# Routing of a decoder trunk's mixture of experts: turning the residual, four rank products, first lists alone, lists of extra tiles between experts

## The chip, the cores and the metric

The kernel runs on one core of one Trainium2 chip. The metric is the device time of one launch in microseconds (us), the median of several runs. One run of the kernel was taken by the hardware profiler; all rows shown here come from it. PE is TensorE's matmul, PEld its weight load, DVE is VectorE, ACT ScalarE, POOL GpSimd; SP only starts DMAs.

## What is computed

One layer of a decoder trunk on 512 tokens (and 16 learned meta tokens ahead of them) of 1024 float32 values each. Three token mixers run side by side, their gated sum goes through an output product, and the result is added to the input. Then comes the part that this case is about:

```python
h = h + merged @ w_out                      # 512 x 1024
u2 = rmsnorm(h, norm_ffn)                   # h * rsqrt(mean(h*h) + eps) * norm_ffn
p_group = softmax(u2 @ wg + bg)             # 4 groups, the best one is taken
e_logits = (u2 @ we + be) of that group     # 8 experts, the best two are taken
e_w = the two best of softmax(e_logits), divided by their sum
y = sum over the two experts: g_val * e_w * (silu(u2 @ w_gate) * (u2 @ w_up)) @ w_down
out = rmsnorm(h + y, norm_final)
```

There are 32 experts with 1024 x 256 gate and up weights and 256 x 1024 down weights, 3 MB each and 96 MB in all. Each token goes to two of them.

## The kernel before, in words

**Order.** Five programs, one an engine, are written out by hand and joined by semaphores. They are a setup (the rows of x normed and turned, small constants as rows that one transpose turns into columns, L220 to L409), the three mixers (up to about 820 us of the span), and `tail()` (from L1592), in three parts: routing, experts, final sum. On each engine the instructions run in the order written. A `Steps` object counts an engine's steps by name; who needs a step waits for its count, so the order of the names is the order of the program.

**Routing, TensorE** (`tensor`, L1660 on). Token tile i (four of 128 tokens) has two output products `o{2i}` and `o{2i+1}`, each 8 matmuls of 512 columns into a PSUM bank of its own (L1684). Behind the products of tile i stand the router's logits of tile i-2 (`logits`, 8 matmuls of 36 columns, L1676) and the transposes of tile i-1 (`turn_tokens`, L1668), which turn rows of `u2`, the normed tokens. Behind the last products stand the transposes of tile 3 and the logits of tiles 2 and 3. The step `lg` is the last. Then come the ranks: which place a token has in its expert's list. A strictly triangular matrix and one of ones are multiplied by the 0/1 choices of each tile, 14 matmuls of 32 columns with the counts of each expert (L1698, L1700, L1702, step `rk`). Then 16 matmuls of 48 columns gather the table of token numbers by slot and by tile of 64 slots (L1708, step `tb`).

**Routing, VectorE** (`vector`, L1736 on). For each tile: add the products to `h` (L1750, 512 columns each), the sum of squares (L1753), mean and eps (L1755), wait for ScalarE's Ln and Exp (L1652, L1654), then the normed rows (L1761), and the copy of turned rows from PSUM to `u2T` (`turned`, L1744). After `lg` stands a chain of about 70 small instructions, each of which waits for the one before (helpers at L1767 to L1777): choice of group and experts up to `M`; ranks and counts read from PSUM; how many extra tiles of 64 rows each expert needs, and where they begin (`j64` to `ob`); places (`A1` to `oh`); eight one-hot matrices of slots (`sl0` to `sl7`, L1838); after `tb` the lists `xe`, `xo`, `xx` of rows to fetch and `yi` of rows to write; owners of extra tiles (`jb` to `ni`); and the weights of the two choices (`gs` to `c2`).

**Routing, queues.** SP starts `w_out`, x once more, the norm rows and the router's weights (L1637 to L1645), the weights of experts 0 to 2, keeps the normed rows of each tile in DRAM (`keep_rows`, L1947, semaphore `rows_kept`), and after `o7` starts the weights of expert 3, the rows of tile 3, and the weights of expert 4. When `rows_kept` shows all four tiles and the last transposes are done it starts the weights of expert 5.

**Experts.** Each expert has one tile of 64 rows; two experts make a pair of 128 rows. GpSimd waits for `rows_kept` and for `xo`, fetches the first two pairs by indirect DMA (L1931), and after `yi` the next two. TensorE turns a pair (L1965), makes gate and up products of an expert (`up`, 32 instructions, L1978), turns the hidden rows (L2013) and makes the down products (`down`, L1985). ScalarE has the sigmoid (L2043) and copies results out (L2049); VectorE copies turned pairs (L2071), gates (L2076, L2080) and copies hidden rows (L2086). GpSimd writes the results to DRAM by indirect DMA (L1937). Weights have six slots. SP loads gate and up of expert e+6 when `up(e)` is done (L1920), and ScalarE's queue loads its down weights after result e (L1923). Extra tiles (more than 64 rows for an expert) would run after all 32 experts, in loops that wait for the step `ni`; with these inputs none runs. The final part reads the results back, adds them weighted by `c_w`, norms and stores.

Of the kernel before, what the change touches and what calls it, by code (L numbers as in the profile page):

```python
# [25 lines left out]
NOWHERE = 65536.0  # L26
# [10 lines left out]
R_NORM, R_LB, R_AN, R_BN, R_CN, R_CONV, R_GKB = 0, 8, 12, 13, 14, 15, 63  # L37
NROWS = 65
# [13 lines left out]
def constants():  # L52
# [16 lines left out]
    j = np.arange(2 * NT)  # L69
    c[:, K_NUM:K_NUM + 2 * NT] = 1 + s + (j // 2 * P + j % 2 * SEQ)  # L70
    c[:, K_HALF] = np.arange(P) // SLOTS - 2
# [30 lines left out]
def hybrid_trunk(nc, x, meta_tokens, norm_mix, w_in, hgrn_lb_logits, hgrn_norm, gdn_conv, gdn_a_log,  # L102
# [4 lines left out]
    with ctx:  # L107
# [111 lines left out]
        def setup_sync(sp):  # L219
            sp.dma_start(xt[:, 0, :], xv[:, 0, :]).then_inc(sem("x_loaded0"), 16)  # L220
            sp.dma_start(C[:, 0:P], consts[:, 0:P]).then_inc(sem("ident_loaded"), 16)
            for at, src in ((R_NORM, norm_mix[0].rearrange("(a b) -> a b", b=P)),
# [3 lines left out]
                            (R_GKB, gla_gk_b[0].rearrange("(a b) -> a b", b=P))):  # L226
# [151 lines left out]
        def setup_tensor(t):  # L378
# [5 lines left out]
            for i in range(NT):  # L384
# [7 lines left out]
                if i == 0:  # L392
                    t.wait_ge(sem("rows_loaded"), 16 * 7)
                    t.transpose(bank(6, NROWS), rowsb, ident[0:NROWS, 0:NROWS]).then_inc(*pe0.did("rows"))
# [1199 lines left out]
        def tail():  # L1594
# [10 lines left out]
            pe2 = Steps(sem("router_pe"), ["o0", "o1", "o2", "o3", "T0", "o4", "o5", "T1", "o6", "o7", "T2", "T3", "lg", "rk", "tb"])  # L1605
            rt = ["lb", "gm", "lt", "ge", "gd", "gx", "og", "el", "es", "m1", "e1", "q1", "x1", "o1",
                  "n2", "m2", "e2", "q2", "x2", "o2", "dm", "O1", "O2", "M", "rank", "cnt",
                  "j64", "xa", "xb", "xc", "xd", "ci", "ob", "A1", "A2", "r1", "r2", "r3", "R1", "R1s", "R2", "R2s",
                  "pos", "pi", "pa", "pm", "tm", "oh"] + [f"sl{n}" for n in range(2 * NT)] + ["tz", "tg", "tx", "xe", "xo", "xx", "ty", "yi", "jb", "jc", "jd", "ji", "ni", "gs", "gv", "w1a", "w1", "w2", "c1", "c2"]
            rows_order = [step_ for i in range(NT) for step_ in ([f"h{2 * i}", f"h{2 * i + 1}", f"s{i}", f"ms{i}"] +  # L1610
                                                         ([f"T{i - 1}"] if i == NT - 1 else []) + [f"u{i}"] +
                                                         ([f"T{i - 1}"] if 0 < i < NT - 1 else []))] + [f"T{NT - 1}"]
            dve2 = Steps(sem("router_dve"), rows_order + rt)
            act2 = Steps(sem("router_act"), [f"{s}{i}" for i in range(NT) for s in ("ln", "rs")] + ["eg", "e2"])
# [32 lines left out]
            def scalar(a):  # L1647
                a.preload_act_table_set("natural_log_exp_and_others")
                for i in range(NT):
                    r = ss2[:, i:i + 1]  # L1650
                    a.wait_ge(*dve2.after(f"ms{i}"))
                    a.activation(r, r, ACT.Ln).then_inc(*act2.did(f"ln{i}"))  # L1652
                    a.wait_ge(*act2.after(f"ln{i}"))
                    a.activation(r, r, ACT.Exp, scale=-0.5).then_inc(*act2.did(f"rs{i}"))  # L1654
# [3 lines left out]
                a.activation(e2, dm, ACT.Exp).then_inc(*act2.did("e2"))  # L1658

            def tensor(t):  # L1660
# [3 lines left out]
                def turn_tokens(i):  # L1664

                    t.wait_ge(*dve2.after(f"u{i}"))
                    for k in range(KD):
                        mm = t.transpose(bank(2 * i + k // 4)[:, k % 4 * P:(k % 4 + 1) * P], u2[:, i, k * P:(k + 1) * P], ident)  # L1668
                    mm.then_inc(*pe2.did(f"T{i}"))

                def logits(i):
                    if i == 0:
                        t.wait_ge(sem("tail_small"), 96)
                    t.wait_ge(*dve2.after(f"T{i}"))
                    for k in range(KD):
# [3 lines left out]


                for i in range(NT):
                    for n in (2 * i, 2 * i + 1):
                        for k in range(KD):
                            mm = t.matmul(bank(n), gates[:, k, i * P:(i + 1) * P], wo[:, k, n % 2 * 512:(n % 2 + 1) * 512],  # L1684
                                          start=(k == 0), stop=(k == KD - 1))
                        mm.then_inc(*pe2.did(f"o{n}"))
                    if i >= 2:
                        logits(i - 2)
                    if i >= 1:
                        turn_tokens(i - 1)  # L1690
                turn_tokens(NT - 1)
                logits(NT - 2)
                logits(NT - 1).then_inc(*pe2.did("lg"))

                t.wait_ge(*dve2.after("M"))
                for i in range(NT):
                    dst = bank(3)[:, i * NX:(i + 1) * NX]
                    t.matmul(dst, strict, mm_[:, i, :], start=True, stop=(i == 0))  # L1698
                    for j in range(i):
                        t.matmul(dst, ones[:, :], mm_[:, j, :], start=False, stop=(j == i - 1))  # L1700
                for j in range(NT):
                    mm = t.matmul(bank(3)[:, NT * NX:(NT + 1) * NX], ones[:, :], mm_[:, j, :], start=(j == 0), stop=(j == NT - 1))  # L1702
                mm.then_inc(*pe2.did("rk"))

                for n in range(2 * NT):
                    t.wait_ge(*dve2.after(f"sl{n}"))
                    for half in range(2):
                        mm = t.matmul(bank(7)[half * SLOTS:(half + 1) * SLOTS, 0:NX + EXTRA], at_slot[:, n, :], at_tile[:, n, :],  # L1708
# [604 lines left out]
```

## Time and profile before

| | us |
|---|---|
| median of 3 runs | 1193.04 (1192.01 to 1194.77) |
| the profiled execution's own time | 1195.24 |
| its span | 1193.3 |
| TensorE busy | 1062.7 (89%) |
| VectorE busy | 482.8 (40%) |
| ScalarE busy | 309.6 (26%) |
| GpSimd busy | 58.9 (5%) |

Mean granted clock of TensorE: 0.952 of full. The span is what the profile's rows count from; the execution's own time is 1.94 us longer. Times in rows are us from the span's start.

### The profile page before, as it was taken

The numbers are of one execution on the slowest core, as the hardware profiler recorded it, in microseconds if no ns is written. First come the engines' busy times: TensorE is split into PE (matmuls) and PEld (weight loads), VectorE is DVE, ScalarE is ACT, GpSimd is POOL, SyncE is SP. The second block draws the span as 40 slices with busy tenths as digits, with TensorE's granted clock in tenths as the row PEclk, the third lists the DMA queues.
The fourth block names the chain that finished last, engine by engine and source line by source line (L and its number), as shares of the span: only waits on it lengthen the run. The fifth ranks groups of instructions, "written<-read, shape, count | busy, mean of one in ns | idle before, by whom it ended". The sixth has DMA issues, their size and how long they took to land.

```text
span 1193.3 us, 15437 instructions
## 1 busy us (share of the span) xinstructions
PE 1062.7 (89%) x6420; PEld 644.6 (54%) x6420; DVE 482.8 (40%) x988; ACT 309.6 (26%) x594; POOL 58.9 (5%) x67
## 2 busy tenths in 40 slices
PE   6999999989999999999989899898993999787870
PEld 5665665665585575675646546443463566444440
DVE  3536464537247256265254345422336212111115
ACT  2535445334233333234223023010000111101012
POOL 0000000000000000000000000000000122111110
PEclk9999999999999999999999899898985899988995
DMA  9222212232132131131122111064545799999965
GB/s 288 68 60 64 54 54 71 54 75 54 36 75 54 53 76 40 50 76 54 36 61 63 53 36 37 1 240 130 234 161 204 278 414 414 415 415 415 416 244 221
DMA packets 111689, 174.34 MB, mean 146 GB/s; under 512 B 8939, under 2 KB 86972, under 8 KB 103298
## 3 DMA queue, kind: packets, MB, share of 16 engines
q1 hardware_dynamic: 98354, 133.29, 32.4%
q10 hardware_dynamic: 7536, 28.90, 6.1%
q0 software_dynamic: 5728, 11.14, 3.8%
q8 instruction: 52, 0.85, 0.3%
q14 instruction: 19, 0.16, 0.0%
HBM read 169.09 MB, written 12.60 MB: 152 GB/s over the span
## 4 chain that ended last, share of the span: by engine, by line
PE 73%; DMA 13%; DVE 10%; ACT 2%; issue 1%; SPq 0%; POOL 0%; DVEq 0%; POOLq 0%
PE ps L732 22%; DMA arena<-in_expert_w_up 11%; PE ps L723 7%; PE ps L729 7%; PE ps L730 7%; PE ps L1978 5%; PE ps L1684 5%; PE ps L777 2%; PE ps L1985 2%; DVE arena L1269 2%; PE ps L756 1%; PE ps L786 1%; PE ps L1676 1%; DVE arena L1502 1%; DVE arena L1499 1%
## 5 line engine op out<-in xcount | busy, mean ns | idle before, releaser
L732 PE MATMUL ps<-arena 128*128 128x512 f32 x672 | 316.1, 606 | 7.2 <-DVE arena L1426 7.2
L732 PEld LDWEIGHTS ps<-arena 128*128 128x128 f32 x672 | 120.2, 191 | 122.8 <-issue 117.8
L729 PE MATMUL ps<-arena 128*128 128x264 f32 x416 | 129.0, 392 | 3.7 <-DVE arena L1426 2.9
L730 PE MATMUL ps<-arena 128*128 128x264 f32 x416 | 127.5, 388 | 0.0
L1978 PE MATMUL ps<-arena,gates 128*64 128x256 f32 x864 | 105.2, 399 | 22.5 <-DMA arena<-in_expert_w_up 21.0
L1269 DVE TENSOR_TENSOR arena<-arena 128x256 f32<-128x256 f32 (+6 forms) x194 | 91.6, 517 | 55.7 <-ACT arena L1090 35.4
L1978 PEld LDWEIGHTS ps<-arena,gates 128*64 128x64 f32 x864 | 64.0, 144 | 71.1 <-DMA arena<-in_expert_w_up 31.6
L723 PE MATMUL ps<-yT,arena 128*128 128x512 f32 x192 | 89.4, 622 | 2.2 <-DVE gates L1341 1.4
L729 PEld LDWEIGHTS ps<-arena 128*128 128x128 f32 x416 | 76.5, 191 | 19.9 <-issue 8.0
L730 PEld LDWEIGHTS ps<-arena 128*128 128x128 f32 x416 | 79.6, 191 | 13.8
L2071 DVE COPY gates<-ps 128x1024 f32<-128x1024 f32 x16 | 19.6, 1225 | 112.9 <-PE ps L1965 112.9
L723 PEld LDWEIGHTS ps<-yT,arena 128*128 128x128 f32 x192 | 37.5, 199 | 48.1 <-issue 47.6
L1684 PE MATMUL ps<-arena,gates 128*128 128x512 f32 x128 | 58.1, 615 | 5.5 <-DVE gates L1269 5.5
L777 PEld LDWEIGHTS ps<-arena 64*64 64x64 f32 x552 | 35.0, 134 | 31.6 <-DVE arena L1502 15.8
L1684 PEld LDWEIGHTS ps<-arena,gates 128*128 128x128 f32 x128 | 25.0, 198 | 37.1 <-issue 30.8
L777 PE MATMUL ps<-arena 64*64 64x64 f32 x552 | 40.5, 222 | 2.5 <-DVE arena L1502 2.4
L2043 ACT ACTIVATE gates<-ps 128x128 f32<-128x128 f32 x32 | 8.9, 278 | 130.2 <-PE ps L1978 130.2
L1985 PE MATMUL ps<-arena,gates 128*64 128x512 f32 x176 | 42.4, 604 | 0.0
L2076 DVE TENSOR_TENSOR gates<-gates,ps 128x128 f32<-128x128 f32 x32 | 9.0, 282 | 77.8 <-ACT gates L2043 77.8
L778 PE MATMUL ps<-arena 64*64 64x64 f32 x552 | 40.5, 222 | 0.0
L1931 POOL DMA_INDIRECT gates<-normed_tokens,gates x16 | 17.0, 1060 | 476.5 <-DVE gates L1774 408.8
L1273 DVE COPY_PREDICATED arena<-C,ps 128x512 f32<-128x512 int32 x56 | 39.6, 719 | 0.0
(327 smaller groups left out, 1281.8 us busy)
## 6 DMA issues: line engine op xcount, KB each, us to landing
arena<-in_w_in SPq DMA_DIRECT2D x68, 512.0 KB, 3.9
arena<-in_expert_w_gate SPq DMA_DIRECT2D x27, 1024.0 KB, 29.0
arena<-in_expert_w_up SPq DMA_DIRECT2D x27, 1024.0 KB, 33.9
arena<-in_expert_w_down ACTq DMA_DIRECT2D x18, 1024.0 KB, 33.1
arena<-in_w_branch SPq DMA_DIRECT2D x12, 512.0 KB, 3.9
C<-in_expert_w_gate SPq DMA_DIRECT2D x5, 1024.0 KB, 33.6
gates<-in_expert_w_up SPq DMA_DIRECT2D x5, 1024.0 KB, 38.9
arena<-in_w_out SPq DMA_DIRECT2D x1, 4096.0 KB, 14.3
```

The costliest lines, as they stand in the source:

```text
L723: mm = t.matmul(merge_bank[b], wt, rhs, start=first, stop=last)
L729: t.matmul(dst[:, 0:HALF], wt, uT[:, k, 0:HALF], start=(k == 0), stop=(k == KD - 1))
L730: mm = t.matmul(dst[:, HALF:], wt, uT[:, k, HALF:], start=(k == 0), stop=(k == KD - 1))
L732: mm = t.matmul(dst, wt, uT[:, k, META:], start=(k == 0), stop=(k == KD - 1))
L777: t.matmul(bank(n)[0:HP, at], lhs[0:HP, lo], rhs[0:HP, lo], start=True, stop=True)
L778: mm = t.matmul(bank(n + 1)[HP:, at], lhs[HP:, hi], rhs[HP:, hi], start=True, stop=True)
L1269: v.tensor_tensor(out_, a_, b2, op).then_inc(*q.did(name))
L1273: v.copy_predicated(tiles(pm), over(up(l).bitcast(I32), NT), tiles(src)).then_inc(*q.did(name))
L1684: mm = t.matmul(bank(n), gates[:, k, i * P:(i + 1) * P], wo[:, k, n % 2 * 512:(n % 2 + 1) * 512], start=(k == 0), stop=(k == KD - 1))
L1978: mm = t.matmul(dst, toks[:, k, :], src, start=(k == 0), stop=(k == KD - 1))
L1985: mm = t.matmul(bank(6 + b)[half * SLOTS:(half + 1) * SLOTS, :], hT[b][:, j * SLOTS:(j + 1) * SLOTS], weights[n][1][:, at:at + 512], start ...
L2071: v.tensor_copy(xT[q % 2], ps[:, 0:2 * 512].rearrange("p (k t) -> p k t", k=KD)).then_inc(pair_read.sem, 1)
```

## The change

- The transposes turn `h`, the residual, in place of the normed rows. The router's weights are multiplied by `norm_ffn` once (step `wn`; the column form comes from one more DMA of 8 rows in the setup, transposed with the others: 73 rows for 65), and the logits by each token's factor after their products (step `sc`). The sum of squares goes from VectorE to ScalarE as `Square` of 1024 columns with an accumulator.
- TensorE's order: `o2`, turn 0, `o3`, `o4`, logits 0, turn 1, `o5`, `o6`, logits 1, turn 2, six of the eight matmuls of `o7`, the first half of turn 3, the other two, logits 2, the second half of turn 3, logits 3 in two halves.
- The normed rows of tile 3 are made after `M`; ScalarE's queue, not SP's, keeps them in DRAM, after `e2`.
- Ranks: one product of 128 columns with the triangular matrix and three with ones, of 96, 64 and 32 columns, for `rk`. The four products of counts go to another bank and step, `ct`, behind it.
- Places: `rk` and `pos` give each choice's rank directly, two instructions `sl0`, `sl1` of 256 columns make the eight one-hot matrices, and the right operand of the table is the 0/1 choices times the token's number (`num`). Ranks of 64 and above match no slot. The table has 32 columns. Lists: `vi`, `xe`, `xo`, `yi`.
- Weights of choices, counts, extra tiles' places and lists stand in the experts' program of VectorE, between its steps; the 16 products of the extra table stand in TensorE's behind the down products of expert 7. ScalarE no longer waits for `ni` ahead of its first sigmoid.

The diff's core:

```diff
-NOWHERE = 65536.0
+NOWHERE = 4 * SEQ
@@ setup_sync
+                            (R_FFN, norm_ffn[0].rearrange("(a b) -> a b", b=P))):
@@ scalar
+                    a.wait_ge(*dve2.after(f"h{2 * i + 1}"))
+                    a.activation(scr2, h[:, i, :], ACT.Square, accum_out=r).then_inc(*act2.did(f"sq{i}"))
...
+                a.wait_ge(*dve2.after(f"u{NT - 1}"))
+                a.dma_start(u2_dram[(NT - 1) * P:, :], u2[:, NT - 1, :]).then_inc(sem("rows_kept"), 16)
@@ tensor
+                out_product(6, every).then_inc(*pe2.did("o6"))
+                logits(1, every, "t1")
+                turn_tokens(2, every, "T2")
+                out_product(7, range(0, KD - 2))
+                turn_tokens(3, low_half, "T3a")
+                out_product(7, range(KD - 2, KD)).then_inc(*pe2.did("o7"))
+                logits(2, every, "t2")
+                turn_tokens(3, high_half, "T3b")
+                logits(3, low_half, "t3a")
+                logits(3, high_half, "t3b").then_inc(*pe2.did("lg"))
...
+                t.matmul(rank, strict, mm_, start=True, stop=False)
+                for i in range(1, NT):
+                    mm = t.matmul(rank[:, i * NX:], ones[:, :], mm_[:, 0:(NT - i) * NX], start=False, stop=(i == NT - 1))
+                mm.then_inc(*pe2.did("rk"))
                 for j in range(NT):
+                    mm = t.matmul(bank(4, NX), ones[:, :], mm_[:, j * NX:(j + 1) * NX], start=(j == 0), stop=(j == NT - 1))
+                mm.then_inc(*pe2.did("ct"))
@@ vector
+                residual(0)
+                residual(1)
+                for i in range(1, NT):
+                    residual(2 * i)
+                    turned(i - 1)
+                    normed(i - 1)
+                    if i == NT - 1:
+                        turned(i, 0)
+                    residual(2 * i + 1)
+                turned(NT - 1, 1)
...
+                tt("num", numbered, by_expert, NUM.unsqueeze(2).broadcast_to([P, 2 * NT, NX]), ALU.mult)
+                normed(NT - 1)
                 v.wait_ge(*pe2.after("rk"))
+                tt("rk", ranked.rearrange("p (k i) e -> p k (i e)", k=2), chosen, over(bank(3, NT * NX), 2), ALU.mult)
+                red("pos", pos, ranked, ALU.add)
+                for k in range(2):
+                    slots_of(f"sl{k}", slice(k * NT, (k + 1) * NT), pos)
                 v.wait_ge(*pe2.after("tb"))
+                held = bank(7, NX)
+                ts("vi", vi, held, -1.0, ALU.mult, float(NOWHERE), ALU.add)
+                ts("xe", xi[0:SLOTS, 0:NX // 2], vi[0:SLOTS, 0:NX:2], WHERE, ALU.bitwise_and)
+                ts("xo", xi[SLOTS:P, 0:NX // 2], vi[SLOTS:P, 1:NX:2], WHERE, ALU.bitwise_and)
+                ts("yi", yi[:, 0:NX], held, -2.0, ALU.mult, C[:, K_HALF:K_HALF + 1], ALU.add)
@@ esync
                 load_weights(sp, 3, 3)
-                keep_rows(NT - 1)
                 load_weights(sp, 4, 4)
                 sp.wait_ge(sem("rows_kept"), 16 * NT)
-                sp.wait_ge(*pe2.after(f"T{NT - 1}"))
+                sp.wait_ge(*pe2.after("T3b"))
                 load_weights(sp, 5, 5)
@@ etensor
                     down(e)
+                    if e == 7:
+                        t.wait_ge(*dve2.after("et"))
+                        for n in range(2 * NT):
+                            for half in range(2):
+                                mm = t.matmul(bank(5)[half * SLOTS:(half + 1) * SLOTS, 256:256 + EXTRA], at_slot[:, n, :], at_tile[:, n, :],
+                                              start=(n == 0), stop=(n == 2 * NT - 1))
+                        mm.then_inc(sem("extra_table"), 1)
@@ evector
+                weights_of_choices()
                 read_pair(0)
+                extra_tiles()
                 read_pair(1)
+                first_extra_tile()
                 hidden(0)
                 hidden(1)
                 read_hidden(0)
...
+                        if e == 7:
+                            extra_lists()
                         hidden(e + 2)
                     read_hidden(e + 1)
+                    if e == 0:
+                        extra_places()
+                    if e == 1:
+                        extra_slots()
+                    if e == 2:
+                        extra_owners()
```

## Rows read from the trace of the kernel before

**Rows 1.** Busy time, granted clock, DMA share, GB/s by stretch: late routing and experts
```profile
core 0: us, PE busy (x) PEld busy (x) DVE busy (x) ACT busy (x) POOL busy (x), PEclk, DMA share, GB/s
910.00:915.00 5.00, 0.00 (x0) 0.00 (x0) 4.42 (x18) 0.00 (x0) 0.00 (x0) 0.50 0.01 2
925.00:930.00 5.00, 3.52 (x18) 2.34 (x18) 1.23 (x1) 0.00 (x0) 0.99 (x1) 0.50 0.21 57
1050.00:1100.00 50.00, 40.48 (x294) 24.40 (x294) 7.27 (x18) 4.41 (x11) 9.11 (x9) 0.86 1.02 415
```

**Rows 2.** Chain of work that ended last (start, us, what): first and last weights
```profile
927.63 5.80 PE ps L1978 x32
...
1109.94 44.00 DMA arena<-in_expert_w_up
```

**Rows 3.** The same chain: transposes and logits beside the output products
```profile
851.28 0.87 PE ps L1668 x8
...
865.89 1.71 PE ps L1676 x16
...
887.36 1.78 PE ps L1668 x8
889.13 6.69 PE ps L1676 x32
```

**Rows 4.** Timeline of VectorE: forms of its steps (start, us, instruction)
```profile
882.28 0.69 DVE L1750 TENSOR_TENSOR yT<-ps,yT 128x512 f32<-128x512 f32 x1 [6.17 <-PE ps L1684]
886.03 1.28 DVE L1761 SCALAR_TENSOR_TENSOR gates<-yT,rw,gates 128x1024 f32<-128x1024 f32 x1
895.85 0.31 DVE L1771 TENSOR_TENSOR rw<-ps,gates 128x144 f32<-128x144 f32 x1 [5.45 <-PE ps L1676]
901.48 0.29 DVE L1771 TENSOR_TENSOR gates<-gates 128x128 f32<-128x128 f32 x1
915.27 0.56 DVE L1771 TENSOR_TENSOR arena<-C,gates 128x384 f32<-128x384 f32 x1
919.02 0.58 DVE L1771 TENSOR_TENSOR gates<-gates 64x16 int32<-64x16 f32 x3
```

**Rows 5.** The chain again: rank products and table
```profile
901.82 1.06 PE ps L1698 x4
...
906.29 1.72 PE ps L1702 x8
...
916.23 2.04 PE ps L1708 x32
```

**Rows 6.** Busy time and clock by stretch, where the clock changes
```profile
884.00:885.00 1.00, 0.85 (x8) 0.61 (x6) 0.51 (x4) 0.41 (x2) 0.00 (x0) 1.00 0.74 303
887.00:888.00 1.00, 0.64 (x4) 0.64 (x5) 0.30 (x1) 0.00 (x0) 0.00 (x0) 0.80 1.00 426
932.00:933.00 1.00, 1.00 (x12) 0.74 (x10) 0.00 (x0) 0.00 (x0) 0.00 (x0) 1.00 0.00 0
```

**Rows 7.** Timeline of SP's queue: rows of tile 3, weights of 5
```profile
887.33 0.33 SPq L1947 DMA_DIRECT2D normed_tokens<-gates  x1
...
895.94 0.33 SPq L1920 DMA_DIRECT2D C<-in_expert_w_gate  x1
```

**Rows 8.** All stores of L1947: issue to landing
```profile
DMA to landing us min/median/max: 2.6/5.6/11.7
```

**Rows 9.** Timeline of GpSimd: the first fetch and the fourth
```profile
920.34 1.46 POOL L1931 DMA_INDIRECT gates<-normed_tokens,gates  x1 [408.75 <-DVE gates L1774]
...
935.29 0.99 POOL L1931 DMA_INDIRECT gates<-normed_tokens,gates  x1 [7.32 <-PE ps L1965]
```

**Rows 10.** DMA issues: landing of all fetches, then of the fourth alone
```profile
DMA to landing us min/median/max: 3.8/9.9/10.9
...
gates<-normed_tokens,gates POOLq DMA_INDIRECT x1, 6.5
```

**Rows 11.** ScalarE's form of the square, in the final part
```profile
L2246 ACT ACTIVATE gates<-yT 128x1024 f32<-128x1024 f32 x4 | 4.2, 1056 | 16.1 <-DVE yT L2233 16.1
```

More of the change, by code:

```diff
@@ L1604, in tail @@
             nfin = gates[:, 22:24, :].rearrange("p a t -> p (a t)")
[L1605 to L1614, printed above, removed]
+            pe2 = Steps(sem("router_pe"), ["o0", "o1", "o2", "T0", "o3", "o4", "T1", "o5", "o6", "T2", "T3a", "o7", "T3b", "lg",
+                                           "rk", "ct", "tb"])
@@ new lines, in tail @@
+            choose = ["sc", "lb", "gm", "lt", "gd", "gx", "og", "el", "es", "m1", "e1", "q1", "x1", "o1",
+                      "n2", "m2", "e2", "q2", "x2", "o2", "dm", "O1", "O2", "M", "num", f"u{NT - 1}"]
+            place = ["rk", "pos", "sl0", "sl1", "vi", "xe", "xo", "yi"]
+            share = ["gs", "gv", "w1a", "w1", "w2", "c1", "c2"]
+            more = [["cnt", "j64", "xa", "xb", "xc"], ["xd", "ci", "ob", "ro", "ri"], ["pi", "pa", "pm", "pd", "pg", "px", "pf"],
+                    ["sx", "jb", "jc"], ["jd", "ji", "ni", "eq", "en", "et"], ["vx", "xx", "yx"]]
@@ L1615, in tail @@
+            rows_order = ["wn", "h0", "h1", "h2", "t0", "u0", "h3", "h4", "t1", "u1", "h5", "h6", "t2", "u2", "t3a", "h7", "t3b"]
+            dve2 = Steps(sem("router_dve"), rows_order + choose + place + share + [n for part in more for n in part])
+            act2 = Steps(sem("router_act"), [f"{s}{i}" for i in range(NT) for s in ("sq", "ln", "rs")] + ["eg", "e2"])
             rw = sb("rw", [P, 900])
@@ L1662, in tensor, with turn_tokens, logits @@
                 t.wait_ge(sem("out_w"), 16)
[L1664 to L1675, printed above, removed]
+                def turn_tokens(i, ks, name):
+                    t.wait_ge(*dve2.after(f"h{2 * i + ks[-1] // 4}"))
+                    for k in ks:
+                        mm = t.transpose(bank(2 * i + k // 4)[:, k % 4 * P:(k % 4 + 1) * P], h[:, i, k * P:(k + 1) * P], ident)
+                    mm.then_inc(*pe2.did(name))
+                def logits(i, ks, copied):
+                    t.wait_ge(*dve2.after(copied))
+                    for k in ks:
                         mm = t.matmul(bank(0)[:, i * 36:(i + 1) * 36], u2T[:, k, i * P:(i + 1) * P], wr[:, k, :],
@@ L1691, in tensor, with out_product @@
-                turn_tokens(NT - 1)
-                logits(NT - 2)
-                logits(NT - 1).then_inc(*pe2.did("lg"))
-                t.wait_ge(*dve2.after("M"))
[L1696 to L1700, printed above, removed]
+                def out_product(n, ks):
+                    i = n // 2
+                    for k in ks:
+                        mm = t.matmul(bank(n), gates[:, k, i * P:(i + 1) * P], wo[:, k, n % 2 * 512:(n % 2 + 1) * 512],
+                                      start=(k == 0), stop=(k == KD - 1))
+                    return mm
```

232 lines of the change are left out of this document (116 added, 116 removed).

## The prediction

> **What bounds the kernel now.** Read the stretches of busy time first [rows 1]. From 1050 to 1100 us the DMA engines are busy the whole time at 415 GB/s while TensorE has gaps (40.5 of 50 us): the experts' weights bound the end. Then the chain of waits [rows 2]: its last weights take 44.0 us from issue to landing, because the queue is full far ahead of use. Where does this stream start? Weights of experts 0 to 5 have slots of their own; those of expert 6 are started when the first gate and up products end, 927.63 + 5.80 = 933.43. Ahead of that the DMA engines have next to nothing to do (2 GB/s from 910 to 915, 57 from 925 to 930) [rows 1]. From 933.4 on the work of the DMA engines is fixed: 26 experts of 3 MB, fetches and results. So the rule for this case is: **each us by which the first up products end earlier is one us off the kernel**, as long as the queue is empty when they end and doesn't run dry afterwards. Before 933.4 the path is output products, turns and logits on TensorE up to 889.13 + 6.69 = 895.82 [rows 3], then small VectorE steps, rank products, the table [rows 5], the first fetch at 920.34 that lands 3.8 us later, at 924.13 [rows 9, 10], and 9.3 us from there to 933.43 (turning, copying, up products).
>
> **Part 1, the end of the logits.** Turn 2 ends at 884.85 (0.85 us busy in 884 to 885, nothing after) [rows 6]. Turn 3 starts at 887.36 [rows 3], because it waits for the normed rows of tile 3: sum of squares, mean, Ln, Exp and 1.28 us of product [rows 4]. In this gap the granted clock falls from 1.00 (2.4 GHz) to 0.50 (1.2 GHz): 0.80 is the mean of 887 to 888 [rows 6]. Turn 3 takes 1.78 us for the 0.87 of turn 0, and two logits 6.69 us for 2 x 1.71 [rows 3]. The new order waits for no normed row. With the same instructions at the full clock and no gap, `lg` comes at 884.85 + 0.87 + 2 x 1.71 = 889.15. Who could be late? `o7` ends 3.9 us ahead of that, at 885.3; its residual add (0.69) [rows 4] ends at 886.0, before logits 2 end at 887.0 and the last half turn wants it. The copy of that half, some 0.65, ends at 888.15, and logits 3 of the first half run until 888.3. ScalarE's square of tile 3, 1.06 us [rows 11] with its read, Ln and Exp some 1.8, ends at 887.8, ahead of `sc`. The `wn` product and the wait for all the router's loads ahead of the first residual delay it by about 5 us; turn 0, which reads it, is behind `o2`, over 8 us later. Gain 6.6 us: `lg` at 889.2.
>
> **Part 2, choice.** `lb` to `M` took 895.85 to 901.78, 5.93 us, with 0.31 for 144 columns from PSUM and 0.29 for 128 [rows 4]. `sc` adds 0.33, the merged `gd` saves 0.21. `M` at 895.3.
>
> **Part 3, ranks.** 28 instructions ran from 901.82 to 908.01: 1.06 for the first four, then 0.215 each (1.72 for eight) [rows 5], at 36, 32 or 128 columns alike: the weight load sets it. Now eight stand ahead of `rk`: 1.06 + 4 x 0.215 = 1.92, so `rk` is ready at 897.25; eight for `ct` end at 898.95. Beside them VectorE makes `num` (256 columns: between 0.29 for 128 and 0.56 for 384 [rows 4], 0.43) and the normed rows of tile 3 (1.28), to 897.05: that is just covered; a warm clock here would save nothing before 897.05.
>
> **Part 4, places and table.** Between the ranks and the table there were 8.2 us on VectorE: copies, counts, three steps of 512 columns, places, one-hots. Left are `rk`, `pos`, `sl0` at 0.45 each, to 898.65, and `sl1` beside the products. The table starts after `ct` at 898.95 and takes 2.04 at most [rows 5]: 901.0. `vi`, `xe`, `xo` at 0.2 to 0.25 (0.58 for three such) [rows 4]: `xo` at 901.7. It was at 919.4. So VectorE's and TensorE's path gives 17.7 us, 6.6 from part 1 and 11.1 from the rest.
>
> **Part 5, what is late next.** The fetches also wait for the rows of tile 3 in DRAM. Their store left SP at 887.33 and the weights of 5, which wait for it, at 895.94 [rows 7]; it had 8.6 us of slack time nobody felt. Now it leaves on ScalarE's queue at 897.05, while the weights of 3 and 4 (6.3 MB from about 886.3, at 415 GB/s until 901.5) are under way. Bounds: 2.6 us on idle engines, 11.7 behind two experts' weights in the same queue [rows 8]. Its own 0.5 MB are 1.3 us; with a half to a third of the bandwidth 1.3 to 2.6 us more, so 3.9 to 5.2. I take 4.9, near the low end, since only a queue of others and nothing in its own is ahead: 902.0. The Trainium skill ("DMA: Bandwidth & Descriptors", Queues, rings and completion order) says that a DMA engine goes round-robin between the queues it has work for, by whole packets; by that rule the store doesn't stand behind the weights, and no row here shows a store on ScalarE's queue.
> On SP, the weights of 3 and 4 leave 3 us later than now, with `o7`; they are wanted 35 us after that.
> GpSimd began 0.9 us after `xo` before (919.4 to 920.34 [rows 9]), so now at 902.9, 17.4 us earlier. But the same store releases the weights of 5, at 902.0 too: 3 MB that ran before while nobody needed the engines now run beside the first fetch. It landed in 3.8 us on idle engines; the fourth, started as the stream began, took 6.5, the median in the full stream is 9.9 [rows 10]. I take 7.0, near the 6.5, since one queue competes: 909.9. This gives back 3.2 us. The weights of 5 end near 912. 9.3 us later than the landing, **919.2**, the first up products end, with the DMA engines idle since 912: 14.2 us earlier than 933.43. I leave these 9.3 alone: the gap before them grows from 5.9 to 9 us, but the clock is low in both, and it rises in the middle of the up products (1.00 in 932 to 933 [rows 6]). All at full clock they would take 3.45, all at half 6.9: -2.3 or +1.1.
>
> **Part 6, what goes between the experts.** Weights of choices, 7 steps, 1.5 us: VectorE waits for the fetch then. Counts to `xc`, 2.3 us: under 5.8 us of up products. `first_extra_tile`, 1.6 us, stands between the copy of pair 1 and `hidden(0)`, which ends at the time at which TensorE finishes up products 1; nothing to 0.3 us of TensorE. `extra_places`, `extra_slots`, `extra_owners`, 1.5 to 2.5 us each, stand where VectorE is idle for 3 to 5 us beside up products. The extra table: 32 instructions, some 1 us on TensorE, in a stretch in which the queue is full. A delay costs only if the queue runs dry: 2 MB per expert last 5.05 us, against 4.7 and 3.9 us between the first ends of up products, later 7.6 against about 6. So nothing; the bound is 0 to 1 us. The setup's row DMA (0.35 us on SP) is some 15 us ahead of the first product that waits for SP's weights: nothing.
>
> **Sum.** 6.6 + 11.1 - 0.3 (store) - 3.2 (fetch beside weights) = 14.2. The profiled execution's own 1195.24 becomes 1181.0. It stood 2.2 above the median of 1193.04, so for the median 1178.8.
>
> **The rivals.** A. *The store is the new wait.* It lands after 11.7 us, as the first did behind 6.3 MB [rows 8], at 908.7; the fetch starts at 909.6 and lands in 6.5 to 9.9, the up products end at 925.4 to 928.8: gain 5 to 8, time 1185 to 1188. For it: 6.3 MB are under way. Against: its own queue is empty. Chance 0.12.
> B. *The clock falls before `lg`.* The last 3.9 us are logits and half turns of few columns. If the clock is at 0.50 from 885.3 on, they take 7.8: gain 10.3, time 1182.7. Against: logits 0 (1.71) and turn 1 ran at the full clock between output products [rows 3]; but that stretch was shorter. The Trainium skill ("TensorE: Matmul & The Clock Gate", Part 4: PE-mode transpose) says that transposes don't count as a busy TensorE the way products do; by it this rival holds if half turns break the activity, and the trace so far shows transposes at full speed. Chance 0.08.
> C. *The fetch is undisturbed*: 3.8 us, gain 17.4, time 1175.6; the weights' data begin 1 us ahead of the fetch's, against it. Chance 0.10.
> D. *No change (0.02)*: the stream isn't set by its start. The empty stretch before 933 speaks against it.
> E. *Slower (0.03).* `hidden(0)` with its wait for `first_extra_tile` breaks TensorE's run, and the clock stays at 0.50 in the experts' stage. An expert takes TensorE about 6.1 us at full clock, 12.2 at half, against 8.4 of the stream (about 220 us for 26): each expert at half clock costs 3.8 us once the lead is used up. From four experts on (15 us) it decides against the 14.2; with six the time is 1193.0 - 14.2 + 22.8 = 1201.6. For it: a gap of 2.5 us cost the clock before turn 3. Against: the same up products brought it back before, with the same gaps around them.
>
> **How the numbers follow.** The forecast (fetch in 5 to 9 us) has 0.65. With A, B, C, D and E that is 1.00. The range takes in C with 1.5 us of a warmer clock, 1174, and the worse half of A, 1187. 0.2% of the time, 2.4 us, is about what a measurement of this kernel can tell from no change; all cases but D and E are beyond it: faster 0.95, same 0.02, slower 0.03.
>
> **What would show it.** Right: no gap over 0.3 us and clock 1.00 on TensorE from 840 to 889; `lg` near 889, `xo` near 902, first fetch started within 1 us of 903 and landed in 6 to 8; first gate load of the stream at 919; GB/s at 415 from 922 on; end of the last weights near 1140. The store's landing tells A, the clock at 885 to 889 B, the clock from 925 to 1000 E. I am wrong if the up products end at 919 and the span isn't 14 us shorter: then the stream is not what sets the end.

## The result and the profile after

The changed kernel takes 1182.92 us in the median of 4 runs (1181.74 to 1183.78), the kernel before 1193.14, also of 4. By the medians that is 10.2 us less, where 14.2 were forecast. The ratio on record, 0.9893 with a 95% interval from 0.9869 to 0.9918, is not the quotient of the two medians (0.9914, which lies in the interval); by it the gain is between 9.8 and 15.6 us. The profiled execution has a span of 1179.9 us for 1193.3, 13.4 less. One profile of each can't be held against medians to a few us: all the code ahead of the first output product takes between 816.8 and 823.7 us from one profile to the next, in both kernels. So the stages are counted from that product from here on. It started at 821.00 before and at 822.06 after.

First the chain of waits of the changed kernel (start, us, what), which answers to [rows 2, 3, 5]:

```profile
822.06 22.65 PE ps L1688 x48
844.71 0.87 PE ps L1675 x8
...
859.32 1.71 PE ps L1681 x16
...
883.43 0.44 PE ps L1675 x4
883.87 1.72 PE ps L1688 x4
885.59 1.71 PE ps L1681 x16
887.30 0.46 PE ps L1675 x4
887.76 1.88 PE ps L1681 x16
...
896.22 1.30 DVE gates L1798
...
897.53 7.43 DMA normed_tokens<-gates
...
905.86 8.10 DMA gates<-normed_tokens,gates
...
917.46 5.53 PE ps L1972 x32
...
1097.67 42.73 DMA arena<-in_expert_w_up
```

There is no gap in TensorE's work until the logits end at 889.64, and the last products and turns are as short as the first (the last logits take 1.88 us for 1.71). Behind the choice of experts the chain no longer goes over ranks and lists: it goes over the store of the rows of tile 3, 7.43 us, and over a first fetch of 8.10 us. The first up products end at 922.99, the last weights land at 1140.40.

The stretches of busy time (columns as in [rows 1]):

```profile
885.00:890.00 5.00, 4.62 (x38) 4.19 (x36) 1.69 (x3) 1.65 (x4) 0.00 (x0) 1.00 0.64 221
890.00:895.00 5.00, 0.00 (x0) 0.00 (x0) 4.31 (x21) 0.42 (x2) 0.00 (x0) 0.55 1.01 421
895.00:900.00 5.00, 4.22 (x29) 4.16 (x30) 4.05 (x9) 1.28 (x1) 0.00 (x0) 0.50 1.02 414
903.00:904.00 1.00, 0.00 (x0) 0.00 (x0) 0.00 (x0) 0.00 (x0) 0.00 (x0) 0.50 1.01 410
904.00:905.00 1.00, 0.00 (x0) 0.00 (x0) 0.01 (x1) 0.00 (x0) 0.00 (x0) 0.50 0.22 86
905.00:910.00 5.00, 0.00 (x0) 0.00 (x0) 1.17 (x7) 0.00 (x0) 2.09 (x2) 0.50 0.77 280
910.00:912.00 2.00, 0.00 (x0) 0.00 (x0) 0.00 (x0) 0.00 (x0) 0.00 (x0) 0.50 0.99 416
916.00:918.00 2.00, 0.54 (x4) 0.41 (x6) 1.84 (x4) 0.00 (x0) 0.99 (x1) 0.50 0.02 8
1050.00:1100.00 50.00, 41.40 (x298) 23.69 (x296) 8.04 (x21) 5.22 (x12) 9.07 (x9) 0.90 1.02 421
```

The clock is at 1.00 until 890, in place of the fall between 887 and 888 [rows 6]. The DMA engines are full until 904 and nearly empty in the next us. The last weights of expert 4 are issued at 888.37 and land 16.8 us later:

```profile
yT<-in_expert_w_down SPq DMA_DIRECT2D x1, 1024.0 KB, 16.8
```

That is 905.2, and the store lands at 904.96, so it is through only when all that had been started before it is through. From 910 to 912, where the first fetch is awaited, the DMA engines are full (416 GB/s); they were empty then before. And the last row of the stretches has something that nothing in the change's text suggests: 421 GB/s in the stream of weights, in which the DMA engines are always busy, for 415 [rows 1].

VectorE's timeline, to be read beside [rows 4]:

```profile
889.66 0.31 DVE L1767 TENSOR_TENSOR rw<-ps,rw 128x144 f32<-128x144 f32 x1 [1.17 <-PE ps L1681]
...
895.76 0.42 DVE L1767 TENSOR_TENSOR gates<-rw,C 128x256 f32<-128x256 f32 x1
896.22 1.28 DVE L1798 SCALAR_TENSOR_TENSOR gates<-yT,rw,gates 128x1024 f32<-128x1024 f32 x1
897.73 0.42 DVE L1767 TENSOR_TENSOR arena<-rw,ps 128x256 f32<-128x256 f32 x1 [0.23 <-PE ps L1716]
...
901.60 0.37 DVE L1770 TENSOR_SCALAR gates<-gates 64x16 int32<-64x16 int32 x2
...
926.92 0.29 DVE L2132 TENSOR_TENSOR gates<-gates,ps 128x128 f32<-128x128 f32 x1
```

`xo` is ready at 901.97, 17.5 us earlier than before. SP's queue and GpSimd wait on, for the store:

```profile
904.98 0.33 SPq L1915 DMA_DIRECT2D C<-in_expert_w_gate  x1
```
```profile
905.86 1.07 POOL L1926 DMA_INDIRECT gates<-normed_tokens,gates  x1 [392.09 <-DVE rw L1770]
```

The view names `L1770`, the line of `xo`, as GpSimd's releaser. But `xo` was done 3.9 us earlier, so it was another: the store, which is no engine's instruction and landed 0.9 us before.

So there are three open points: how much of each part of the change arrives at the end, what holds the first fetch, and where 421 GB/s come from.

### The profile page after: what moved, and what is told of

Same layout as the page of the kernel before. It is cut to its first block, busy times and chain, and to the rows that moved or that the text cites. A ratio compares the mean times of both kernels' runs of the same rounds, so it can differ in the third digit from the quotient of the medians.

```text
span 1179.9 us, 15475 instructions
## 1 busy us (share of the span) xinstructions
PE 1058.0 (90%) x6440; PEld 641.1 (54%) x6440; DVE 477.3 (40%) x971; ACT 314.6 (27%) x602; POOL 58.5 (5%) x67
## 4 chain that ended last, share of the span: by engine, by line
PE 74%; DMA 14%; DVE 9%; ACT 1%; issue 1%; SPq 0%; POOL 0%; DVEq 0%; POOLq 0%
PE ps L732 22%; DMA arena<-in_expert_w_up 11%; PE ps L729 8%; PE ps L723 7%; PE ps L730 7%; PE ps L1972 6%; PE ps L1688 5%; PE ps L777 2%; PE ps L1979 2%; DVE arena L1269 2%; PE ps L756 1%; PE ps L786 1%; PE ps L389 1%; DVE arena L1502 1%; DVE arena L1499 1%
## 5 line engine op out<-in xcount | busy, mean ns | idle before, releaser
L2050 ACT ACTIVATE gates<-ps 128x512 f32<-128x512 f32 x32 | 19.1, 597 | 71.1 <-PE ps L1979 71.1
```

## The experiments

All kernels are the changed one with one edit, except where the kernel before is named. Read from their profiles, in us from the first output product to within 0.1 us (the stream is the time from the end of the first up products to the landing of the last weights; GB/s from 1025 to 1075):

| run | first product | logits end | first fetch | first up products end | stream | GB/s |
|---|---|---|---|---|---|---|
| before | 821.00 | 74.8 | 99.3 | 112.4 | 220.5 | 415 |
| e1, before again | 822.72 | 74.8 | 99.4 | 112.6 | 220.2 | 415 |
| after | 822.06 | 67.6 | 83.8 | 100.9 | 217.4 | 421 |
| e5, after again | 822.92 | 68.4 | 84.8 | 102.2 | 217.7 | 421 |
| e2, normed rows turned | 820.20 | 74.2 | 87.5 | 100.4 | 217.6 | 422 |
| e3, ten rank products | 823.74 | 68.4 | 85.1 | 102.5 | 217.6 | 422 |
| e4, extras first | 822.87 | 68.4 | 89.9 | 103.0 | 218.0 | 422 |
| e6, before, shifted | 818.10 | 74.5 | 99.0 | 111.8 | 217.7 | 421 |
| e7, after, shifted | 822.48 | 68.3 | 84.8 | 102.2 | 220.1 | 416 |
| e8, weights of 5 after the fetch | 821.83 | 68.4 | 85.1 | 98.3 | 219.7 | 421 |
| e9, rows before the choice | 823.37 | 68.4 | 81.7 | 99.2 | 217.5 | 421 |
| e10, e8 and e9 | 819.84 | 67.9 | 81.1 | 94.2 | 218.9 | 420 |
| e11, all slots aligned | 816.78 | 67.7 | 84.2 | 101.2 | 217.1 | 422 |
| e12, e10 and e11 | 823.58 | 68.4 | 81.6 | 94.9 | 217.2 | 422 |

The logits' end varies by 0.8 us with the time for which the first output products run at half the clock: the first 48 instructions take 22.65 us in the changed kernel's profile, where the clock is back at 1.00 from 826 us, and 23.48 in e3 and e4; in e3 it is still at 0.50 from 826 to 828. e1 to e4 were run once each, the profiled time (1197.85, 1180.88, 1185.14 and 1186.25 us), so they speak by their stages alone. e5 to e8 ran on one chip, e9 to e12 on another, beside 21 and 11 runs of the kernel before (medians 1196.99 and 1194.30); their ratios are those on record, and differ by up to 0.0025 from the quotients of the medians, which lie inside the intervals.

**e1: the kernel before again.** No edit.

> The kernel before once more, for its stages. Both theories: first up products end at 933.4 within 0.3 us, since that part is compute in a fixed order. What is open is the stream behind it: in the profile of before the last weights landed 220.5 us after that point (415 GB/s), in the changed kernel's 217.4 us (420 GB/s). If the rate belongs to the run and not to the kernel, this run shows another value between 216 and 222; if the change made the stream faster, this one shows 220.5 again.

112.6 and 220.2 us, at 415 GB/s. The slower stream belongs to the kernel, not to the run. The up products ended at 935.27, not at 933.4 within 0.3: 1.7 of these 1.8 us lie ahead of the first output product, which the expectation had taken as fixed.

**e2: the first part undone.** Normed rows are turned, in the order of before. With that the store is back on SP's queue, as soon as its rows are made and not behind the choice of experts; so e2 undoes two things, and not the turning alone.

```diff
-                    t.wait_ge(*dve2.after(f"h{2 * i + ks[-1] // 4}"))
+                    t.wait_ge(*dve2.after(f"u{i}"))
-                        mm = t.transpose(..., h[:, i, k * P:(k + 1) * P], ident)
+                        mm = t.transpose(..., u2[:, i, k * P:(k + 1) * P], ident)
...
+                keep_rows(NT - 1)
                 load_weights(sp, 4, 4)
```

> The changed kernel with its first part undone: normed rows are turned in the old order, the store of tile 3 leaves SP's queue as soon as the rows are made. Theory W (the store and the weights of expert 5 hold the first fetch): logits end near 897.2 instead of 889.6, xo near 909.5, but the store has landed and the weights of 5 are in by then, so the fetch lands in about 4 us, near 914.3; first up products end near 923.5, 0.5 us later than in the changed kernel (922.99). Rival S (the parts add up): they end 7.5 us later, at 930.5.

The logits end 6.7 us later, counted from the first product, and the first up products 0.5 us *earlier* than in the changed kernel (100.4 for 100.9). The chain of e2:

```profile
907.74 3.34 DMA gates<-normed_tokens,gates
...
914.56 6.04 PE ps L1962 x32
```

Its weights of expert 5 left SP at 894.20, 8.4 us behind the store, and were in when the fetch began; the fetch took 3.34 us, not 8.10. The two rows, SP's and that of the DMA engines as the fetch begins:

```profile
894.20 0.33 SPq L1904 DMA_DIRECT2D C<-in_expert_w_gate  x1
```
```profile
907.00:908.00 1.00, 0.00 (x0) 0.00 (x0) 0.43 (x4) 0.00 (x0) 0.27 (x1) 0.50 0.11 45
```

Theory W holds: in the changed kernel the whole gain of the first part is spent waiting for the store and sharing the engines.

**e3: ten rank products.**

```diff
-                t.matmul(rank, strict, mm_, start=True, stop=False)
-                for i in range(1, NT):
-                    mm = t.matmul(rank[:, i * NX:], ones[:, :], mm_[:, 0:(NT - i) * NX], ...)
+                for i in range(NT):
+                    dst = rank[:, i * NX:(i + 1) * NX]
+                    mm = t.matmul(dst, strict, mm_[:, i * NX:(i + 1) * NX], start=True, stop=(i == 0))
+                    for j in range(i):
+                        mm = t.matmul(dst, ones[:, :], mm_[:, j * NX:(j + 1) * NX], ...)
```

> The changed kernel with ten rank products of 32 columns ahead of rk in place of four. rk is ready 2.6 us later, xo at 904.6 instead of 901.97. Theory W: the store lands at 904.96 either way, the fetch starts at 905.9, first up products end at 923.0, no change. Rival S: 925.6.

From the logits' end the first fetch starts 16.7 us on for 16.4 in e5, and the first up products end 34.1 for 33.8. `xo` comes 2.6 us later behind the logits (14.9 for 12.3), and that costs 0.3: it fits under the store.

**e4: extra tiles' work ahead of the first lists.** The five functions that the change put between the experts, and the weights of choices, are called in the router's program before the wait for `tb`.

```diff
+                weights_of_choices()
+                extra_tiles()
+                first_extra_tile()
+                extra_places()
+                extra_slots()
+                extra_owners()
                 v.wait_ge(*pe2.after("tb"))
```

> The changed kernel with weights of choices, counts, extra places and owners back on VectorE ahead of the first lists. About 9.8 us of VectorE more: xo near 909.9 instead of 901.97. Theory W: the fetch starts near 910.8, overlaps only the end of the weights of 5 and lands near 915.5; first up products end near 924.7, 1.7 us later than in the changed kernel. Rival S: 7.9 us later, 930.9.

`xo` comes 20.5 us behind the logits, 8.2 later than in e5, the fetch starts 5.1 later, and the first up products end 34.6 behind them for 33.8: 0.8 us of cost, where 1.7 had been expected. The chain shows where the rest went, into a quick fetch:

```profile
912.74 4.42 DMA gates<-normed_tokens,gates
```

So three large parts, undone one at a time, cost -0.5, 0.3 and 0.8 us. That doesn't make them worthless: what hides each of them is the wait for the store and for the weights of 5, and e9 and e10 below take that wait away. None of the three was undone there, so what each is worth without the wait is not shown.

**e5: the changed kernel again.** No edit.

> The changed kernel once more. Its setup ends between 820 and 824 us in the runs so far, so the stages are counted from the first output product: up products end 100.9 later, last weights land 217.5 after that. In the five profiles so far the two of the kernel before took 220.3 and 220.5 us for the second stretch at 415 GB/s, the changed kernel and three variants of it 217.4 to 218.0 at 421. Theory P (place in SBUF): the change widens the tile of turned rows from 65 to 73 columns, and every tile allocated behind it moves from 224 to 0 bytes past a multiple of 256. With it the gain against before is some 13 to 14 us; without the stream's part 10 to 11.

Stream 217.7 us, at 421 GB/s, as expected. The first up products came at 102.2, not 100.9, with 0.8 of it from the clock of the first products and 0.4 from that of the up products (5.90 us for 5.53). The median of 6 runs is 1183.73, the ratio 0.9907 (0.987 to 0.9943).

**e6 and e7: the places in SBUF.** The change makes the tile `rowsT` 73 columns wide for 65. Tiles are allocated one behind the other, so that `gates`, `yT` and `arena`, which hold the weights' slots, start 32 bytes further on: 0 bytes past a multiple of 256 in place of 224. e6 gives that shift to the kernel before, e7 takes it from the changed one. The edit to the kernel before, then that to the changed one:

```diff
-        rowsT = sb("rowsT", [P, NROWS])
+        rowsT = sb("rowsT", [P, NROWS + 8])[:, 0:NROWS]
```
```diff
-        rowsT = sb("rowsT", [P, NROWS])
+        rowsT = sb("rowsT", [P, NROWS + 56])[:, 0:NROWS]
```

> The kernel before with nothing but 8 unused columns behind the tile of turned rows, so that gates, yT and arena start at a multiple of 256 bytes. Theory P: 421 GB/s, last weights 217.5 us after the first up products end, time 3 us (0.25%) below the kernel before. Rival Q (lists, order or code of the new routing make the stream faster): 415 GB/s, 220.4 us, no change.

> The changed kernel with 56 unused columns there, so that the same tiles start 224 bytes past a multiple of 256, as in the kernel before. Theory P: 415 GB/s, 220.4 us, 3 us slower than the changed kernel; rival Q: 421 GB/s, 217.5 us. The first up products end 100.9 us after the first output product in both.

Of each the two ends of the stream (the first up products and the last weights, by the chain) and a busy row, first e6, then e7:

```profile
924.43 5.44 PE ps L1978 x32
...
1104.38 43.15 DMA arena<-in_expert_w_up
```
```profile
1025.00:1075.00 50.00, 41.95 (x304) 24.12 (x301) 8.05 (x21) 5.24 (x12) 9.10 (x9) 0.90 1.02 421
```
```profile
918.91 5.78 PE ps L1972 x32
...
1101.85 42.95 DMA arena<-in_expert_w_up
```
```profile
1025.00:1075.00 50.00, 41.90 (x302) 23.61 (x302) 8.05 (x21) 5.24 (x12) 8.86 (x9) 0.90 1.02 416
```

The rate goes with the shift in both directions: 217.7 us for the kernel before, 220.1 for the changed one; of the fourteen profiles the three at 415 or 416 GB/s are those with the old places. Ratios to the kernel before are 0.9948 (0.9921 to 0.9975) for e6 and 0.992 (0.9895 to 0.9945) for e7; e7's median is 2.9 us above that of e5, which ran beside it. e6's median is 6.0 us below that of the kernel before, for the 3 expected; its profile shows 3 of them in the stream, and where the rest comes from is not shown. Eight unused columns gave the kernel before 3 us of stream, and this is shown: it is part of the change's gain, by accident.

**e8: weights of expert 5 after the first fetch.**

```diff
                 sp.wait_ge(*pe2.after("T3b"))
+                sp.wait_ge(sem("pair_x0"), 16)
                 load_weights(sp, 5, 5)
```

> The changed kernel with the weights of expert 5 started when the first fetch has landed instead of beside it. Theory W: the fetch has the engines for itself and lands in 3.4 to 4.4 us instead of 8.1, the first up products end 97.0 us after the first output product instead of 100.9, the weights of 5 run in the empty stretch before them; 4 us (0.3%) faster than the changed kernel. Rival (the fetch is slow for the store's or its own sake): it takes 8 us and nothing changes, or the weights of 5 run into the stream and cost what they gave.

The chain of e8:

```profile
898.09 7.89 DMA normed_tokens<-gates
...
906.88 3.43 DMA gates<-normed_tokens,gates
...
913.80 6.33 PE ps L1973 x32
```

The fetch takes 3.43 us, the first up products end 3.9 us earlier than in e5. Theory W holds for the fetch. But the stream is 2.0 us longer, so that half of it is lost. The issues between 905 and 925 show where: the weights of 5 now run beside the next fetches, and the last of them, issued at 911.23, land 11.1 us later at 922.3, 2.2 us behind the end of the first up products, when the stream should have had the engines for itself:

```profile
C<-in_expert_w_gate SPq DMA_DIRECT2D x1, 1024.0 KB, 6.3
gates<-in_expert_w_up SPq DMA_DIRECT2D x1, 1024.0 KB, 9.0
gates<-in_expert_w_down SPq DMA_DIRECT2D x1, 1024.0 KB, 11.1
```

The time, 1181.31 in 4 runs, ratio 0.986 (0.9795 to 0.9926), can't be told from e5's.

**e9: rows of tile 3 before the choice.** VectorE idles for 1.2 us ahead of the logits' end; the normed rows are made there, and ScalarE's queue starts the store at once.

```diff
                 turned(NT - 1, 1)
+                normed(NT - 1)
...
-                normed(NT - 1)
```

> The changed kernel with the normed rows of tile 3 made, and their store started, ahead of the choice of experts instead of behind it (VectorE waits for the logits there anyway; the choice starts at most 0.15 us later). Theory W, counted from the end of the logits: the store lands 7.5 to 8 us after 0.2, ahead of xo, the first fetch starts at +13.3 instead of +16.3; the weights of 5 now follow those of 4 without a gap and still run beside it, so it takes 7 to 8 us; first up products end 3 us earlier. Rival (VectorE's and TensorE's chain to xo is what holds the fetch): no change.

SP's timeline of e9, then its chain:

```profile
900.68 0.33 SPq L1915 DMA_DIRECT2D C<-in_expert_w_gate  x1
```
```profile
905.02 8.60 DMA gates<-normed_tokens,gates
```

The store left at 891.82 and had landed by 900.68, 8.9 us later (7.5 to 8 expected); the fetch starts 13.3 us behind the logits, and with the weights of 5 beside it takes 8.60 us. The first up products end 3.0 us earlier than in e5. Median 1179.03, ratio 0.9861 (0.9835 to 0.9888). The rival, that the chain to `xo` holds the fetch in the changed kernel, falls: that chain is as long here, 12.3 us from the logits' end. Here, with the store out of the way, it is what the fetch waits for.

**e10: both.**

> The same, and the weights of expert 5 wait for the first fetch to land. Theory W: fetch from +13.3 in 3.4 to 4 us, first up products end at +26.3 from the logits' end instead of +33.8; the weights of 5 end 1 to 2 us behind that and cost the stream as much (219.6 for 217.6 in e8); last weights 5.5 us earlier than in the changed kernel. If W is wrong on the order of things and the stream were bound by all bytes since the output products, nothing would come of it beyond e8's 1.9.

```profile
900.98 3.52 DMA gates<-normed_tokens,gates
...
907.99 6.03 PE ps L1973 x32
```

Fetch at 13.3 from the logits, 3.52 us; first up products at 26.3 from there, stream 218.9. The last weights land 313.1 us from the first product, for 319.9 in e5: 6.8 us, of which 0.5 is the clock of the first products. Median 1175.80 in 4 runs, ratio 0.984 (0.9811 to 0.9869), against 0.9907 and 0.9893 of the changed kernel.

**e11 and e12: every slot at a multiple of 256 bytes.** In the changed kernel only some of the slots are: 0, 3 and the apart one (gate and up of slot 4, in the arena) start 240 bytes past a multiple, and the gate slot among the constants 128. Below is the core of e11's edit.

```diff
+        front_pad = sb("front_pad", [P, 32])
...
-        rowsT = sb("rowsT", [P, NROWS])
+        rowsT = sb("rowsT", [P, NROWS + 32])[:, 0:NROWS]
...
-        ARENA = 29500
+        ARENA = 29504
...
-            free = arena[:, 2 * 3 * 2 * D:2 * 3 * 2 * D + 828]
+            free = arena[:, 2 * 3 * 2 * D:2 * 3 * 2 * D + 832]
-            apart = arena[:, 2 * WX + 828:ARENA]...
+            apart = arena[:, 2 * WX + 832:ARENA]...
```

> The changed kernel with every weight slot at a multiple of 256 bytes: the arena is 4 columns longer (slots 0 and 3 and the apart slot started 240 bytes past one) and 32 columns stand ahead of the constants (the slot in them started 128 past one). Theory P: half of the weights' bytes were still out of place in the changed kernel; 424 to 428 GB/s, stream 213.5 to 215.5 us for 217.6. The Trainium skill (DMA: Bandwidth & Descriptors, How a descriptor splits into AXI transactions) counts by its rule 2.2% fewer beats from the kernel before to the changed one, of which 1.3 show in the stream, and 1.8% more from there to here. Rival: only the step from 224 to 0 counted: 421 GB/s and 217.6.

> The two of e10 and the slots of e11. If all add up: 5.5 + 3 = 8.5 us below the changed kernel, last weights 94.6 + 216.5 us after the first output product; time 1175 beside 1183.7.

e11, the stretch that had 415 and 421:

```profile
1025.00:1075.00 50.00, 41.44 (x300) 23.88 (x297) 7.69 (x21) 5.25 (x12) 9.11 (x9) 0.90 1.02 422
```

422 GB/s and 217.1 us, for the 213.5 to 215.5 expected: a miss. The step from 224 to 0 bytes gave 3 us, that of the other slots to 0 gave 0.3 to 0.6. The rival, that only the first step counted, is as near as one profile tells. In e12 the stream is 217.2 us for e10's 218.9, of which part may be chance. e12's median of 1177.43 in 6 runs (1167.94 to 1181.10), ratio 0.9834 (0.9799 to 0.9869), is not distinguishable from e10's. Neither ran beside the changed kernel; from the first output product to the last weights they are 6.8 and 7.8 us ahead of e5, and by their ratios both are faster than the kernel before. Their intervals end at 0.9869, where those of the changed kernel begin (0.9869 and 0.987).

## Why the prediction was right, and where it was not

**The bound** was read rightly: the end moves with the end of the first up products. In the profile of after these come 11.5 us earlier from the first output product, and the queue didn't run dry behind them (420 GB/s from 950 to 1100). e9, where they come 3.0 us earlier than in e5, has its last weights 3.2 us earlier; e8 shows the rule's condition at work, since with the weights of 5 still under way half of the 3.9 us is lost. The rule's second half, that the work of the DMA engines from there on is fixed, was wrong by 3.1 us, in the kernel's favour: the bytes are fixed, their rate isn't. e6 and e7 show that it goes with the place of the tiles. Nothing in the prediction looked at what a wider tile does to those behind it.

**Parts 1 to 4** came out nearly to the digit. `lg` was forecast 68.2 us from the first product, and it is 67.6; the clock stayed at 1.00, so rival B fell. The Trainium skill ("TensorE: Matmul & The Clock Gate", Part 4: PE-mode transpose) says that a transpose doesn't count as a busy PE the same way. Here the half turns, 0.44 and 0.46 us between products, did not cost the clock; whether longer transposes would, no run here shows. `lg` to `xo` took 12.33 us for the forecast 12.5.

**Part 5 is where the sum was off.** The mechanism was there, its sizes weren't. The store took 7.43 us for 4.9, the fetch 8.10 for 7.0, and the weights of 5 beside it did that, as e8 shows (3.43 without them). Together that is 3.6 us too little, so that "- 0.3 (store)" should have been -2.8 and "- 3.2 (fetch beside weights)" -4.3; 0.9 came back, since the logits ended 0.6 earlier and the up products 0.3 sooner behind the landing, and 11.5 of the forecast 14.2 was left. I had taken the store near the low end of its bounds because its own queue was empty; 7.4 to 7.9 us in the seven profiles that start it there say that traffic in another queue holds it up nearly as much as traffic ahead of it in its own (8.6 us on SP's queue in the kernel before, 8.4 in e2). The prediction also had the weights of 3 and 4 through at 901.5. The engines were full until 904, and the store landed within 0.3 us of the last of these weights here, in e5 and in e8 (905.0 and 905.2, 906.8 and 906.7, 906.0 and 905.8). An estimate from the bytes gives the same: 6.8 MB with the store's, from about 887.5 at 415 GB/s, are 16.4 us, to 904. Why the store stays to the end of that traffic isn't shown. The Trainium skill ("DMA: Bandwidth & Descriptors", Queues, rings and completion order) has the engines go round-robin between queues. A store of 8.9 us in e9, issued 1.3 us behind the last weights of 4, neither contradicts nor proves it. The shares of a half or a third, from which I worked out 3.9 to 5.2 us, were too large. Rival A was half true: the store is the new wait, by 3.0 us and not by 7.

**The terms are no prices.** The sum adds 6.6 for part 1 and 11.1 for parts 2 to 4. Undone alone, the first part, with its store moved back too, costs -0.5 us (e2), the rank products' 2.6 us cost 0.3 (e3), and the extras' work 0.8, not the 5.1 us by which the fetch starts later (e4). The prediction did compare `xo` (901.7) with the store (902.0) and went on from the later one. But it had them 0.3 us apart, so that each us on the chain to `xo` seemed to be one off the kernel; measured, they are 3.0 apart, and the fetch is short once the weights of 5 are through. A total can come out near with all parts made together, and still not tell what any of them is worth.

**Part 6** held. `hidden(0)` starts at 926.92, ends by 927.53, and the up products of expert 1 end at 927.67; no gap, and no clock lost (rival E). The extra table's 32 instructions took 0.89 us on TensorE while the queue was full. Rival C, the undisturbed fetch, did not occur by itself, but it is what e8 and e10 make.

**The total**: -11.5 (up products) -3.1 (stream) +1.1 (first product later) +0.1 (end) = -13.4 us between the two profiled spans. The medians differ by 10.2. With first products that start anywhere in 7 us, one profile of each can't settle the difference; what part of these 3 us is chance stays open. The median of 1182.92 lies in the range and 4.1 us above the forecast of 1178.8, and luck has a share in that: 3 us of the gain are the stream's, which the prediction had at nothing. e7, the changed kernel without them, took 1186.66, near the range's end.

## What to carry to other kernels

Where several things release one instruction, don't add what is saved on each path: write down the times at which all of them are ready, and take the latest, again after each saving. A store or a load that was started in time because its release was early becomes part of the path when the chain beside it gets shorter, and may be cheap to move: here rows made in 1.2 us in which VectorE waited anyway, and one wait of SP, were worth some 6 us (e10, without the 0.5 of the clock). Check too when the traffic already under way will be through: the store, started late into it, landed with the last of it. And in a stage bound by DMA, look at where the tiles start in SBUF, and after a change of any tile's width look again: compare the rates in GB/s before explaining a gain by what was meant.

## What the runs showed of the hardware that was not expected

- Loads into tiles that start 224 bytes past a multiple of 256 ran at 415 or 416 GB/s, into the same tiles 32 bytes on at 421: 1.2 to 1.4%, in both kernels and both directions, 220.1 to 220.5 us of stream for 217.4 to 217.7. The Trainium skill ("DMA: Bandwidth & Descriptors", How a descriptor splits into AXI transactions) says that a descriptor that doesn't start at a multiple of 256 bytes costs extra beats. The page words this for what a transaction reads; here the side that is out of place is the one written. By its count (an estimate, with the 8 KB of a gate or up row and the 4 KB of a down row as descriptors) this shift saves 1.7% of the beats, not the 2.2% of e11's expectation, and aligning all slots 1.8% more. e6 and e7 have the right sign and three quarters of the size, but e11 had to give as much once more and gave 0.2%. So that a shift of 32 bytes matters is shown; that the 256-byte rule is the reason is not, and why the slots at 240 and 128 cost so little is open.
- A store of 0.5 MB takes 2.6 us on idle engines [rows 8], 7.4 to 7.9 when it is started 10 us into 6.3 MB of another queue (seven profiles), and 8.6 to 8.9 when it is started right behind their issue (e9, e10, e12). A fetch of one pair takes 3.3 to 3.5 us alone in e2, e8, e10 and e12 (3.8 to 3.9 in the kernel before, e1 and e6) and 8.0 to 8.6 beside one expert's weights.
- One and the same kernel, the one before, took from 1187.29 to 1200.03 us in 21 runs on one chip, and the code ahead of the first output product ended between 816.8 and 823.7 us in 14 profiles. Mean granted clocks of those 21 runs ran from 0.949 to 0.962, and the runs of more than 1197 us had 0.949 to 0.953.
